# Down stages with 6 and 7 of 22 seven-product pairs, three buffers for h's mixed parts, high-part products first, three seven-product pairs in each dilated head

## What is computed

```python
def reference(x, ...):
    h = x
    for i in range(DEPTH):                       # DEPTH = 2
        y = rmsnorm(h, ln_mix[i])
        if i % 2 == 0:
            h = h + diff_attention(y, a_w_qkv[0], ..., a_w_o[0], rel_bias, i)
        else:
            h = h + dilated_attention(y, b_w_qkv[0], ..., b_w_o[0], rel_bias)
        h = h + conv_ffn(rmsnorm(h, ln_ffn[i]), f_w_up[i], f_conv_w[i], f_conv_b[i], f_w_down[i])
    return h

def conv_ffn(h, w_up, conv_w, conv_b, w_down):   # w_up 2048 x 11264, w_down 5632 x 2048
    u = causal depthwise convolution of h @ w_up, width 3, + conv_b
    gate, val = jnp.split(u, 2, axis=-1)
    return (jax.nn.silu(gate) * val) @ w_down
```

## Time and profile before

| | us |
|---|---|
| median of 3 runs | 2523.66 (2522.17 to 2524.38) |
| the profiled execution's own time | 2522.48 |
| its span, first to last instruction | 2520.7 |
| PE busy | 2512.4 (11913 matmuls) |
| DVE busy | 2009.2 |
| ACT busy | 1403.5 |
| DMA queues, share of 16 engines | 56.6% for the weights |
| one head, from one head's entry 7 to the next's | 72.26 |

### The profile page before, as it was taken

One profiled execution on the slowest core, in us unless ns is written; L12 is line 12 of the kernel. 1 busy time (PEld: TensorE's weight loads), 2 busy tenths in 40 slices (PEclk: granted clock), 3 DMA queues, 4 the chain that ended last, 5 costly groups with the idle time before them and its releaser, 6 DMA issues.

```text
span 2520.7 us, 33147 instructions
## 1 busy us (share of the span) xinstructions
PE 2512.4 (100%) x11913; PEld 2104.8 (84%) x11913; DVE 2009.2 (80%) x2265; ACT 1403.5 (56%) x1519; POOL 28.9 (1%) x36
## 2 busy tenths in 40 slices
PE   9999999999999999999999999999999999999999
PEld 8888888888888888888888888888888888888887
DVE  6656666898888998987677777766688888899897
ACT  5545554666666555556445545444566666655554
POOL 1000000000000000000000000000000000000000
PEclk9999999999999999999999999999999999999999
DMA  8544554646465556566555666554464645546654
GB/s 280 183 159 158 189 186 157 211 167 232 150 227 172 184 200 217 187 210 202 159 166 177 178 192 193 176 167 153 148 234 150 229 170 194 201 161 225 215 167 156
DMA packets 362188, 471.72 MB, mean 187 GB/s; under 512 B 18997, under 2 KB 215813, under 8 KB 361968
## 3 DMA queue, kind: packets, MB, share of 16 engines
q1 hardware_dynamic: 360448, 465.64, 56.6%
q0 software_dynamic: 1408, 4.76, 0.6%
q10 hardware_dynamic: 240, 0.10, 0.0%
HBM read 468.31 MB, written 3.68 MB: 187 GB/s over the span
## 4 chain that ended last, share of the span: by engine, by line
PE 92%; DVE 4%; ACT 2%; DMA 1%; issue 1%; SPq 0%; ACTq 0%; DVEq 0%
PE psum L1951 21%; PE psum L1953 21%; PE psum L1952 21%; PE psum L1843 8%; PE psum L1841 8%; PE psum L1842 8%; DVE w_lo L1126 2%; PE psum L2006 1%; ACT w_hi L672 1%; PE psum L2124 1%; DVE xT L1475 1%; DMA w_raw<-in_f_w_down 1%; PE psum L1781 0%; PE psum L1822 0%; PE psum L2088 0%
## 5 line engine op out<-in xcount | busy, mean ns | idle before, releaser
L1951 PE MATMUL psum<-w_hi,xT 128*128 128x512 f32 x2214 | 867.7, 392 | 1.2 <-DVE xT L1475 0.4
L1953 PE MATMUL psum<-w_hi,xT 128*128 128x512 f32 x2214 | 862.0, 389 | 0.0
L1952 PE MATMUL psum<-w_lo,xT 128*128 128x512 f32 x2214 | 861.6, 389 | 0.0
L672 ACT ACTIVATE w_hi<-w_raw 128x2048 fp32r<-128x2048 f32 (+1 forms) x328 | 599.9, 1831 | 400.9 <-PE psum L1953 304.4
L1126 DVE TENSOR_TENSOR w_lo<-w_raw,w_hi 128x2048 fp32r<-128x2048 f32 (+1 forms) x328 | 708.1, 2180 | 127.3 <-ACT w_hi L672 127.3
L1951 PEld LDWEIGHTS psum<-w_hi,xT 128*128 128x128 f32 x2214 | 415.7, 188 | 90.8 <-DVE xT L1475 5.4
L1953 PEld LDWEIGHTS psum<-w_hi,xT 128*128 128x128 f32 x2214 | 415.6, 188 | 86.8
L1952 PEld LDWEIGHTS psum<-w_lo,xT 128*128 128x128 f32 x2214 | 415.8, 188 | 84.8
L1841 PE MATMUL psum<-w_hi,xT 128*128 128x512 f32 (+1 forms) x992 | 365.1, 368 | 0.3 <-DVE phase L1605 0.3
L1843 PE MATMUL psum<-w_hi,xT 128*128 128x512 f32 (+1 forms) x992 | 359.5, 362 | 0.0
L1842 PE MATMUL psum<-w_lo,xT 128*128 128x512 f32 (+1 forms) x992 | 358.9, 362 | 0.0
(11 more groups left out here) (202 smaller groups left out, 1994.0 us busy)
## 6 DMA issues: line engine op xcount, KB each, us to landing
w_raw<-in_f_w_up SPq DMA_DIRECT2D x352, 512.0 KB, 5.0
w_raw<-in_f_w_down SPq DMA_DIRECT2D x176, 512.0 KB, 5.1
w_raw<-in_b_w_qkv SPq DMA_DIRECT2D x192, 256.0 KB, 3.7
w_raw<-in_a_w_qkv SPq DMA_DIRECT2D x94, 512.0 KB, 4.5
w_raw<-in_b_w_qkv SPq DMA_DIRECT2D x256, 128.0 KB, 2.8
w_raw<-in_a_w_o SPq DMA_DIRECT2D x16, 1024.0 KB, 5.4
w_raw<-in_b_w_qkv SPq DMA_DIRECT2D x32, 512.0 KB, 5.3
w_raw<-in_b_w_o SPq DMA_DIRECT2D x16, 1024.0 KB, 5.2
```

Of the source, the lines that this page charges most:

```text
L672: nc.scalar.activation(w_hi[:, slot, cols], w_raw[:, slot, cols], ACT.Copy).then_inc(hi_ready, 1)
L1951: pe.matmul(o, xh, hi, start=start, stop=False)
L1952: pe.matmul(o, xh, lo, start=False, stop=False)
L1953: return pe.matmul(o, xl, hi, start=False, stop=stop)
```

## The change

1. **Down stages.** The groups have two or three pairs. Pass 0 has six plain pairs and groups of 2, 2, 3, 3, 2, 3; pass 1 three plain pairs and groups of 3, 2, 2, 3, 3, 2, 3. That makes 6 and 7 seven-product pairs (5 and 6 before), and 57 entries (55).
2. **Buffers.** `mixT` and `h_mix` hold three pairs' activation sums, so the sums for one seven-product pair wait for the one three before it.
3. **Dilated heads.** Pairs 4, 5 and 6 have seven products (4 and 6 before), 15 entries, the order below; the loops over the heads are written out on PE, ACT and DVE. PE waits for the previous head's transposed weights at the first "one" and for its output at the first "sum".
4. **High parts first.** PE waits for the high part, makes all products of the chunk with it (two thirds), then waits for the low part and makes the rest. The last chunk of each pass of a down stage and the first pair of a dilated head keep the old order.

```diff
-    end = plain + 3 * groups
-    for j in range(plain, end, 3):
-        order += [("one", j), ("std", j + 1), ("sum", j), ("std", j + 2)]
-    order += [("std", j) for j in range(end, PAIRS)]
+    j = plain
+    for size in groups:
+        order += [("one", j), ("std", j + 1), ("sum", j)] + [("std", j + i) for i in range(2, size)]
+        j += size
+    order += [("std", i) for i in range(j, PAIRS)]
...
-DOWN_ENTRIES = [(what, p, j) for p, form in enumerate(((6, 5), (3, 6))) for what, j in down_pass(*form)]
-B_ENTRIES = tuple(("all", j) for j in range(4)) + ENTRIES
+DOWN_ENTRIES = [(what, p, j) for p, form in enumerate(((6, (2, 2, 3, 3, 2, 3)), (3, (3, 2, 2, 3, 3, 2, 3)))) for what, j in down_pass(*form)]
+B_FAST = (4, 5, 6)
+B_ENTRIES = tuple(("all", j) for j in range(4)) + (
+    ("std", 0), ("std", 1), ("std", 2), ("one", 4), ("std", 3), ("sum", 4), ("one", 5), ("sum", 5), ("one", 6), ("sum", 6),
+    ("std", 7))
+MIX_PAIRS = len(B_FAST)
...
             def h_mix_high(layer, f):
 
-                if f > 1:
-                    chunk_used(act, DN0[layer] + DOWN_FAST[f - 2] + 2)
+                if f >= MIX_PAIRS:
+                    chunk_used(act, DN0[layer] + DOWN_FAST[f - MIX_PAIRS] + 2)
...
-                if mixes_made(layer, f) > 2:
-                    dve.wait_ge(h_mix_lo, mixes_made(layer, f) - 2)
+                if f >= MIX_PAIRS:
+                    dve.wait_ge(h_mix_lo, mixes_made(layer, f - MIX_PAIRS))
...
-                    split_ahead(c, e, h, turn)
-                    if e + LEAD + 2 == B_ONES[0]:
-                        b_add_weights(c + B_ONES[0], c + B_SUMS[0], turn)
-                    if e + LEAD + 3 == B_ONES[1]:
-                        b_add_weights(c + B_ONES[1], c + B_SUMS[1], turn)
+                    if e + LEAD + 1 == B_ONES[0]:
+                        b_add_weights(c + B_ONES[0], c + B_SUMS[0])
+                    split_ahead(c, e)
+                    for one, to in zip(B_ONES[1:], B_SUMS[1:]):
+                        if e + LEAD + 3 == one:
+                            b_add_weights(c + one, c + to)
...
-            b_head(B0, 0, 0)
-            with pe.Fori(0, H // 2 - 1) as t:
-                for i in (1, 2):
-                    b_head(B0 + i * B_HEAD, t * 2 + i, i % 2, t)
-            b_head(B0 + (H - 1) * B_HEAD, H - 1, 1)
+            for h in range(H):
+                b_head(B0 + h * B_HEAD, h, h % 2)
...
+            def plain_square(c, x, own, start, stop, high_made, low_made):
+
+                high_made()
+                for half, i, tile in SQUARE:
+                    for m in range(M):
+                        high(x[i], m, c, tile, psum[:, own + 2 * half + m, :], start and i == 0)
+                low_made()
+                for half, i, tile in SQUARE:
+                    for m in range(M):
+                        ins = low(x[i], m, c, tile, psum[:, own + 2 * half + m, :], stop and i == 1)
+                ins.then_inc(used, 1)
```

More of the change, by code:

```diff
@@ L96, with fast_of @@
 END = DN0[1] + DOWN
-assert all(x % SLOTS == 0 for x in (A_HEAD, 2 * B_HEAD, 2 * UP))
+assert all(x % SLOTS == 0 for x in (A_HEAD, H * B_HEAD, 2 * UP))
+def fast_of(n):
+    return B_FAST if n == 2 else FAST
 def up_entry(c):
@@ L1944, in out_proj, with high, low @@
                         transpose_resid(n, j - 8)
+            def high(x, m, c, tile, o, start=False):
+                hi = part_of(w_hi, c % SLOTS, 512 * tile, 512)
+                for h in range(2):
+                    pe.matmul(o, x[:, h, P * m:P * (m + 1)], hi, start=start and h == 0, stop=False)
+            def low(x, m, c, tile, o, stop=False):
+                return pe.matmul(o, x[:, 0, P * m:P * (m + 1)], part_of(w_lo, c % SLOTS, 512 * tile, 512), start=False,
+                                 stop=stop)
             def product(x, m, c, tile, o, start=False, stop=False):
@@ new lines, in fast_sum @@
+            def fast_sum(c, x, mix, own, other, start, stop, high_made, low_made):
+                high_made()
+                high(mix[1], 0, c, 2, psum[:, other + 1, :], start)
+                high(mix[2], 0, c, 1, psum[:, other + 2, :], start)
+                high(mix[0], 0, c, 0, psum[:, other + 3, :], start)
+                high(x[1], 1, c, 3, psum[:, own + 1, :])
+                low_made()
+                low(mix[1], 0, c, 2, psum[:, other + 1, :], stop)
+                low(mix[2], 0, c, 1, psum[:, other + 2, :], stop)
+                low(mix[0], 0, c, 0, psum[:, other + 3, :], stop)
+                low(x[1], 1, c, 3, psum[:, own + 1, :]).then_inc(used, 1)
@@ L2135, in b_entry_of @@
                 x = [xT[:, 2 * j + i, :, :] for i in range(2)]
-                if what == "std":
-                    def taken():
+                if what == "std" and j == 0:
+                    low_made()
+                    upper_first(c, x, own, h)
+                elif what == "std":
+                    plain_square(c, x, own, False, 2 * j + 2 == KB, high_made, low_made)
+                else:
+                    i = B_FAST.index(j)
+                    mix = [mixT[:, s, i, :, :] for s in range(4)]
+                    (fast_one if what == "one" else fast_sum)(c, x, mix, own, other, i == 0, i == len(B_FAST) - 1,
+                                                              high_made, low_made)
@@ L2138, in taken, with upper_first @@
+            def upper_first(c, x, own, h):
+                for half, tiles in ((1, (0, 3)), (0, (1, 2))):
+                    if half == 0:
                         pe.wait_ge(b_raw_act, h + 1)
                         pe.wait_ge(b_raw_dve, h + 1)
-                    upper_first(c, x, own, j == 0, 2 * j + 2 == KB, taken if j == 0 else None)
-                else:
-                    i = FAST.index(j)
-                    mix = [mixT[:, s, i, :, :] for s in range(4)]
-                    (fast_one if what == "one" else fast_sum)(c, x, mix, own, other, i == 0, i == len(FAST) - 1)
@@ L2147, in upper_first @@
[L2147 to L2151 removed]
                     for i, tile in enumerate(tiles):
                         for m in range(M):
[L2154 to L2155 removed]
+                            ins = product(x[i], m, c, tile, psum[:, own + 2 * half + m, :], i == 0, False)
```

230 lines of the change are left out of this document (112 added, 118 removed).

## The result

The changed kernel took 2545.4 us (median of five runs, 2543.3 to 2547.1), the kernel before, run beside it, 2522.2 (2521.9 to 2524.4). The ratio is 1.009, 95% interval 1.0079 to 1.0101. The forecast was 2533, so the direction was right and the size was not: +23.2 us where +9.7 were expected. The profiled execution took 2543.3 with a span of 2541.5, and is held against that of before, 2522.5 with 2520.7.

What follows compares the result with a forecast made beforehand. The prediction took PE to bound the kernel: -8.2 -3.9 +21.3 +0.5 = +9.7 on the profiled 2522.5 gave 2532.2, and 1.2 for the median made 2533.4, said as 2533. The range was 2528 to 2546.

Steps and rivals of the forecast that it cites:

- Bound: Whole kernel: PE is the bound, busy all but 8 us of the span, at 0.2267 us per matmul.
- part 1: Down stages and dilated heads: 36 matmuls removed at 0.2267 us each, 8.2 us saved with nothing hidden.
- Part 2: Down stages: groups of two move DVE's additions into the chain; ten old pauses go, -3.9 us, six new ones add 21.3.
- the six places: Entries 20, 35 and 49 of each down stage: PE waits about 3.4 us for split_h, 3.55 with slow matmuls behind.
- The clock: Rival, 5 in 100: in the six down-stage pauses PE's clock falls, 2.2 us each, 13 in all, giving 2546.
- The sign that the prediction gave for a full clock: Profile page after the change: the granted clock row, in 40 slices, would read full.
- Elsewhere in the down stages: Rest of DVE's down-stage queue: groups of two lose at most 2.6 us of a three-chunk lead; PE finds low parts ready.
- Part 3: High parts first: a low part may come 3.6 us later, but this saves nothing and costs 0.
- Part 4: Dilated heads: each 0.68 us shorter, 72.26 to about 71.6; 0.5 us lost for all heads; written-out loops 0.
- the gating chunk: End of a dilated head: the chunk whose low part b_combine follows, estimated up to 0.4 us late.
- the spare: End of a dilated head: b_combine was done 0.9 us before PE needed it, which covers a delay of 0.4.
- the old pause of 0.4 in the last head: Last dilated head: PE already pauses, due 1698.46, come 1698.87; its going was the lower bound, -0.4.

Runs made afterwards that it cites:

- adds_behind_split: Changed kernel with only the three additions put behind the split of h's block at entries 22, 37 and 51 of each down stage, mix_h staying ahead; 2519.9 us.
- both_behind_split: Changed kernel with the additions and mix_h put behind the split of h's block at entries 22, 37 and 51 of each down stage; 2516.4 us.
- order_only: Kernel before with only high parts' products first and the dilated heads' loops written out; old down lists, two seven-product chunks per head, two buffers; 2522.9 us.
- split_first: Changed kernel with the split of h's block first in its entry on ACT and DVE, mix_h and additions later, first head's mix_low behind b_take; 2512.8 us.
- old_down_lists: Changed kernel with the groups of the down passes as before, five and six groups of three; 2519.5 us.
- pause_filled: Changed kernel with 28 matmuls by a tile of zeros ahead of PE's wait for the split in the six pauses; 2534.9 us.
- doses: Kernel before with DVE repeating the split's subtraction one to four times at the ten tight blocks, lengthening PE's pauses; 2560.0 us in one run.

## Why the prediction was right in direction and wrong in size

**Bound and part 1** (36 matmuls, 8.2 us): right. The up stages, which have no pause, keep their pace.

**Part 2, the six places:** right, in place, number and size. They lie 87, 155 and 212 us into the down stage (forecast 87, 154, 209; the later ones are pushed back by the slow matmuls before them), five of them 3.38 us over pace and one 3.53, with DVE's queue in the order read from the listing. adds_behind_split gave 2.6 for the additions, and both_behind_split 0.54 for `mix_h`.

**The clock: the step that failed.** It stood among the rivals with 5 in 100 and "against: no row", and the forecast kept the clock full: the matmuls behind a pause were priced at 0.14 us, where the trace shows another 1.6 behind five of the six. That no row of the kernel before spoke for it was no argument, since PE never stood for 1 us there: the trace had nothing to say. The one stretch that did show the lower level was the start, with PE just come out of idleness. The rival's time, 2546, is the one that came (2545.4), but partly by luck: it had 2.2 us for each of six pauses, 13 in all, the profile shows 1.6 for each of five, 7.9 in all, and the rest of the difference came from small pauses that the rival didn't have. The Trainium skill ("TensorE: Matmul & The Clock Gate", HAM oscillation — how this bites in real kernels) has waits between groups of matmuls put PE back to half clock; the trace agrees, with 0.58 to 0.61 behind five of the six pauses, and the prediction named that rule and gave it too little weight. The forecast pause and the fallen clock were written as rivals, where the second follows from the first, so the term belonged in the sum. The sign that the prediction gave for a full clock, the row of the page, came out full all the same: five stretches of a few us don't show in slices of 63.5.

**Elsewhere in the down stages:** the claim that PE finds everything else in time holds in layer 0. In layer 1 it broke once, for 1.1 us, because it priced the additions by their duration and not by the load that they wait for. The additions waited 2.12 us for the load of `w_down`, and the split of the block stood behind them; the prediction had looked at loads in the heads only.

**Part 3:** 0, as forecast (order_only). What was missed is its use: it gives the low part slack, and split_first spends that slack on the split.

**Part 4:** in the changed kernel heads 1 and 2 came out 71.68 us apart, 72.26 less 0.58, and the six distances between heads 1 and 7 are 71.60 to 72.00 (72.26 - 0.68 = 71.58 was forecast):

```profile
1251.54 1.05 PE L1939 MATMUL psum<-w_hi,xT 128*128 128x512 f32 x3
```

```profile
1323.22 0.58 PE L1939 MATMUL psum<-w_hi,xT 128*128 128x512 f32 x1
```

0.5 us was taken for all heads; the medians of old_down_lists give 2.0 (5.4 saved by 24 matmuls, 2522.9 - 2519.5 = 3.4 seen), within their noise, and PE's starts in its trace 1.6. 1.2 of it is the first head's queue of `b_take`, which wasn't looked at: the prediction followed the end of a head and not the wider `mix_low` at its beginning. PE also waits for the combine in two heads (0.5 and 0.3 us), and the old pause of 0.4 in the last head is gone. For the combine the mechanism was named (the gating chunk late by up to 0.4, "which the spare covers"), and the spare did not always cover it.

By parts, from the medians: 9.7 as forecast and 13.5 on top. Of these the clock has some 8 to 10 (7.9 in the profiled execution, 10.5 at most by pause_filled), the first head 1.2 and the place in layer 1 1.1; the rest isn't told apart, and how the 13.5 divide in an unprofiled run can't be told more exactly.

## What to carry to other kernels

When an edit moves work into the queue of a helper engine, list what stands between the event that frees a buffer and the instruction that PE waits for, and put that instruction first: here the same lists of chunks are 23 us slower or 12 us faster than before by nothing but the order of a few instructions. Price a pause of PE of about 3 us with the clock behind it (here 1.4 to 3 us more, behind eleven of the twelve pauses of 2.8 to 5.3 us), and treat "the trace has never shown it" as no evidence when the trace never had the condition. An instruction that waits for a load is priced by the load, and nothing urgent should stand behind it.

## What the runs showed of the hardware

The slow matmuls began with the restart in four of eleven cases, all in doses, and 0.3 to 1.5 us behind it in the others, so the first matmuls of a resumed PE may be fast and the next ones slow. In the kernel before with longer pauses all six of 2.8 us and more had the half clock behind them, in the changed kernel five of six of 3.4; the four of 1.5 us, and the six of 0.8 in adds_behind_split, had it full. A page that shows the clock in 40 slices doesn't show any of this; the step between two starts does (0.427 against 0.227 us). Multiplications by a tile of zeros, 28 in 3.5 us, kept the clock full through all six pauses of pause_filled. Why the sixth pause of the changed kernel left it full stays open; nothing here was run to tell that.
